# Low-rank products, token mixing, key norms and bonus sums move into the input projection of a one-core decoder step

## What is computed

```python
h = rmsnorm(x, norm1) * (1 + sc1) + sh1
proj = h @ w_in                       # 2048 x 5656
p_rkv = proj[..., RKV_OFF:GATE_OFF]   # 3 x 1024 columns; p_rkv_prev is the row before
rkv = p_rkv + mu_rkv * (p_rkv_prev - p_rkv)
r, k, v = split(rkv, 3)
xx = h_shift - h                      # h_shift: the row before, state_shift for the first
xw, xa, xg = (h + xx * mu_wag[i] for i in range(3))
w_log = -softplus(-(decay_w0 + tanh(xw @ decay_w1) @ decay_w2)) - 0.5
decay = exp(-exp(w_log))
a = sigmoid(iclr_a0 + (xa @ iclr_a1) @ iclr_a2)
g = sigmoid(xg @ gate_g1) @ gate_g2
kk = heads(k * k_k); kk = kk / max(sqrt(sum(kk * kk)), 1e-12)
k = k * (1 + (a - 1) * k_a)
# scan over tokens with r, decay, k, v, kk, a; then
bonus = sum(r * k * r_k, per head) * v
```

## Time and profile before

| | us |
|---|---|
| median of 3 runs | 2838.94 (2838.39 to 2849.66) |
| profiled execution, own time | 2834.51 |
| its span, first to last instruction | 2832.1 |
| mean granted TensorE clock | 0.902 |

### The profile page before, as it was taken

One profiled execution on the slowest core, in us unless ns is written; L12 is line 12 of the kernel. 1 busy time (PEld: TensorE's weight loads), 2 busy tenths in 40 slices (PEclk: granted clock), 3 DMA queues, 4 the chain that ended last, 5 costly groups with the idle time before them and its releaser, 6 DMA issues. The chain is left out here.

```text
span 2832.1 us, 48973 instructions
## 1 busy us (share of the span) xinstructions
PE 2373.7 (84%) x21091; PEld 1728.0 (61%) x21091; DVE 780.7 (28%) x1996; ACT 297.8 (11%) x681; POOL 77.9 (3%) x119
## 2 busy tenths in 40 slices
PE   5999998599999536776576698689999999999996
PEld 4677676377777426674564476556656666566664
DVE  0211211300000584445466502411211221112215
ACT  0101100100000210001142200100100011100001
POOL 0000000000000100000101100100000000000000
PEclk9999999599999756767588899699999999999998
DMA  5888884433331312001376820699999999999991
GB/s 213 336 303 311 338 301 183 165 117 121 118 119 59 63 41 96 5 5 34 67 229 241 314 107 1 271 425 422 427 417 425 426 422 426 418 423 427 421 420 54
DMA packets 182404, 687.45 MB, mean 243 GB/s; under 512 B 38810, under 2 KB 39787, under 8 KB 142667
## 3 DMA queue, kind: packets, MB, share of 16 engines
q1 hardware_dynamic: 172002, 640.42, 57.5%
q0 software_dynamic: 7056, 38.29, 4.0%
q10 hardware_dynamic: 3220, 6.86, 0.6%
HBM read 687.09 MB, written 19.86 MB: 250 GB/s over the span
## 5 line engine op out<-in xcount | busy, mean ns | idle before, releaser
L2498 PE MATMUL bank<-sb_gate_w,sb_x_picked 128*64 128x256 f32 x2048 | 331.6, 389 | 51.4 <-DMA sb_up_w<-in_w_up_dram 51.4
L571 PE MATMUL bank<-sb_hT,sb_w_in 128*128 128x296 f32 x1408 | 353.7, 415 | 3.9 <-PEq L462 3.9
L2498 PE MATMUL bank<-sb_up_w,sb_x_picked 128*64 128x256 f32 x2048 | 330.7, 388 | 0.0
L571 PEld LDWEIGHTS bank<-sb_hT,sb_w_in 128*128 128x128 f32 x1408 | 269.0, 191 | 88.6 <-issue 6.0
L2498 PEld LDWEIGHTS bank<-sb_gate_w,sb_x_picked 128*64 128x64 f32 x2048 | 175.9, 140 | 122.7 <-issue 78.2
L2523 PE MATMUL bank<-sb_down_w,sb_hiddenT 128*64 128x512 f32 x1024 | 226.8, 594 | 9.0 <-ACT sb_x_picked L2580 9.0
L397 PE MATMUL bank<-sb_cmp_xT,sb_cmp_w 128*128 128x254 f32 x1024 | 223.4, 379 | 6.7 <-ACT sb_cmp_xT L213 5.8
L397 PEld LDWEIGHTS bank<-sb_cmp_xT,sb_cmp_w 128*128 128x128 f32 x1024 | 193.2, 190 | 39.0 <-ACT sb_cmp_xT L213 8.4
L2498 PEld LDWEIGHTS bank<-sb_up_w,sb_x_picked 128*64 128x64 f32 x2048 | 179.5, 140 | 49.1 <-issue 0.6
L2650 DVE TENSOR_TENSOR sb_hidden<-sb_hidden,bank 128x256 f32<-128x256 f32 x32 | 13.5, 421 | 679.4 <-ACT sb_hidden L2588 679.4
L2523 PEld LDWEIGHTS bank<-sb_down_w,sb_hiddenT 128*64 128x64 f32 x1024 | 84.1, 137 | 128.9 <-issue 115.4
(11 more groups left out here) (543 smaller groups left out, 2480.1 us busy)
## 6 DMA issues: line engine op xcount, KB each, us to landing
sb_gate_w<-in_w_gate_dram SPq DMA_DIRECT2D x64, 2048.0 KB, 16.6
sb_up_w<-in_w_up_dram SPq DMA_DIRECT2D x64, 2048.0 KB, 20.9
sb_down_w<-in_w_down_dram SPq DMA_DIRECT2D x64, 2048.0 KB, 17.7
sb_w_ada<-in_w_ada_dram SPq DMA_DIRECT2D x48, 2048.0 KB, 10.8
sb_w_in<-in_w_in_dram SPq DMA_DIRECT2D x11, 4096.0 KB, 13.2
sb_cmp_raw<-in_cache_cmp_kv_dram SPq DMA_DIRECT2D x128, 256.0 KB, 7.6
sb_sample_kv<-in_w_out_dram SPq DMA_DIRECT2D x16, 1024.0 KB, 11.1
sb_sample_kv<-in_state_win_kv_dram SPq DMA_DIRECT2D x8, 1024.0 KB, 13.8
```

The source lines that it names most:

```text
L571: ins = pe.matmul(k.bank[m][:, 0:NX], w[r][:, t, m * P:(m + 1) * P], k.hT[:, t, :], start=(t == 0), stop=(t == KT - 1))
L2498: ins = pe.matmul(bank[b][64 * half:64 * half + 64, col:col + 256], x[:, t, b * 64:b * 64 + 64], w[i][:, t % CK, half * 256:half * 256 + 256],
```

## The change

`phase_lora`, `phase_rkv` and the last-rows block go; their work moves into `phase_in`, whose stage now ends at the scan.

- Weight chunks have 256 columns (2 MB, two tiles), still in two buffers; the 24 r, k, v tiles come first, the other 20 after, with 288 columns.
- Mixing h before a product is replaced by scaling the matrix: x @ W with x = (1 - mu) h + mu h_shift becomes h @ ((1 - mu) W) plus the shifted columns of h @ (mu W). DVE scales the down matrices, PE does four groups of 16 products, DVE adds the shifted part.
- For r, k, v ACT writes (1 - mu) times the tile, DVE adds mu times the neighbouring columns straight from PSUM.
- High products, sums of squares, bonus sums and the branch gates stand between tiles in PE's list; key norms, reciprocals and bonus run one tile of 288 columns at a time on ACT and DVE.
- The samples' states are loaded into the first weight buffer once its last tiles are done, and transposed at the end of the stage. The scan's masks run in the same stage.
- Buffers are shared with tiles that are not in use yet. 39 semaphores more belong to the set that `phase_rows` clears.

The core of the diff:

```diff
+def w_in_column(n):
+    blocks = RKV_TILE // 2
+    return (n + blocks if n < 3 * RT // 2 else n - 3 * RT // 2) * 2 * P
...
+                sp.dma_start(r1[0][:, :, 0:64], view("decay_w1")).then_inc(s_l1, 16)
+                sp.dma_start(r1[0][:, :, 64:128], view("iclr_a1")).then_inc(s_l1, 16)
+                sp.dma_start(r1[1], view("gate_g1")).then_inc(s_l1, 16)
+                for tile, name in zip(w2, ("decay_w2", "iclr_a2", "gate_g2")):
+                    sp.dma_start(tile, A[name][0]).then_inc(s_l2, 16)
+                sp.wait_ge(s_lr, 4)
+                sp.dma_start(A["shift_prompt"][0], last_rows[0:1, :]).then_inc(s_lo, 16)
+                sp.dma_start(A["shift_sample"][0], last_rows[1:NC, :]).then_inc(s_lo, 16)
+                for n in range(2, N_CH):
+                    sp.wait_ge(s_tile, 2 * n - 2)
+                    sp.dma_start(w[n % 2][:, :, :], w_view[:, :, w_in_column(n):w_in_column(n) + 2 * P]).then_inc(s_w[n % 2], 16)
+                    if n == 2:
+                        sp.dma_start(wg[:, :, :], w_view[:, :, GATE_OFF:IN_W]).then_inc(s_wg, 16)
+                sp.wait_ge(s_tile, N_T - 2)
+                for b in range(NB):
+                    sp.dma_start(k.state_rows[b // 2][64 * (b % 2):64 * (b % 2) + 64, :].rearrange("i (h j) -> i h j", j=64),
+                                 A["state_wkv"][0, b].rearrange("h i j -> i h j")).then_inc(s_states, 16)
...
+                def tile(j):
+                    n, ch = j // 2, k.w_in[j // 2 % 2]
+                    pe.wait_ge(s_w[n % 2], 16 * (n // 2 + 1))
+                    if 4 <= j < N_R + 4:
+                        pe.wait_ge(s_mix, j - 3)
+                    elif j >= N_R + 4:
+                        pe.wait_ge(s_copy[j % 2], (j - 4 - N_R) // 2 + 1)
+                    wide = NX if j < N_R else NT
+                    for t in range(KT):
+                        ins = pe.matmul(bank[j % 4][:, 0:wide], ch[:, t, j % 2 * P:(j % 2 + 1) * P], hT[:, t, 0:wide],
+                                        start=(t == 0), stop=(t == KT - 1))
+                    ins.then_inc(s_tile, 1)
...
+                def low_rank():
+                    pe.wait_ge(s_lr, 4)
+                    for i in range(4):
+                        pe.wait_ge(s_wm, i // 2 + 1)
+                        wide = NX if i % 2 else NT
                         for t in range(KT):
+                            ins = pe.matmul(bank[4 + i][:, 0:wide], (r1, m1)[i % 2][i // 2][:, t, :], hT[:, t, 0:wide],
                                             start=(t == 0), stop=(t == KT - 1))
...
+                def squares_summed(t):
+                    pe.wait_ge(s_sq, t + 1)
+                    pe.wait_ge(s_ha, 2 * RT)
+                    pe.wait_ge(s_hd, RT)
+                    if t >= 4:
+                        pe.wait_ge(s_mx, t - 3)
+                    pe.matmul(bank[4 + t % 4][:, 0:NT], k.headones[:, :], k.bonus[:, t, :], start=True, stop=True).then_inc(s_n, 1)
...
+                def states_turned():
+                    pe.wait_ge(s_states, 16 * NB)
+                    pe.wait_ge(s_gc, len(ROWS))
+                    for p in range(2):
+                        pe.wait_ge(s_copy[p], (N_T - N_R) // 2)
+                    for pair in range(NB // 2):
+                        for t in range(RT):
+                            ins = pe.transpose(bank[2 * pair + t // 4][:, (t % 4) * P:(t % 4 + 1) * P],
+                                               k.state_rows[pair][:, t * P:(t + 1) * P], k.ident[:, :])
+                        ins.then_inc(s_turned, 1)
+                for j in range(N_T):
+                    tile(j)
+                    if j == 0:
+                        last_turned()
+                    elif j == 3:
+                        low_rank()
+                    elif 8 <= j < 20:
+                        high(2 * (j - 8))
+                        high(2 * (j - 8) + 1)
+                    elif 20 <= j < 28:
+                        squares_summed(j - 20)
+                    elif 30 <= j < 38:
+                        bonus_summed(j - 30)
+                    elif j == 40:
+                        branch_gates()
+                states_turned()
...
+                def own_part(j):
+                    act.wait_ge(s_tile, j + 1)
+                    act.activation(k.rkvT[:, j, 0:NT], bank[j % 4][:, 0:NT], ACT.Copy, scale=om[:, j:j + 1]).then_inc(s_ev, 1)
...
+                def keys(t):
+                    act.wait_ge(s_mix, RT + t + 1)
+                    kk_gain = k.par[:, C_KK + t:C_KK + t + 1]
+                    act.activation(k.kk[:, t, :], K[:, t, :], ACT.Copy, scale=kk_gain)
+                    act.activation(k.bonus[:, t, :], K[:, t, :], ACT.Square, scale=kk_gain).then_inc(s_sq, 1)
+                    act.activation(k.y[:, t, :], k.a[:, t, :], ACT.Identity, bias=oka[:, t:t + 1],
+                                   scale=k.par[:, C_KA + t:C_KA + t + 1]).then_inc(s_t2, 1)
+                def root(t):
+                    act.wait_ge(s_mx, t + 1)
+                    act.activation(k.y[:, t, :], k.y[:, t, :], ACT.Sqrt).then_inc(s_rt, 1)
...
+                for j in range(N_T):
+                    if j < N_R:
+                        own_part(j)
+                    elif j % 2 == 0:
+                        act.wait_ge(s_tile, j + 1)
+                        act.copy(k.pT[:, j - N_R, 0:NT], bank[j % 4][:, 0:NT]).then_inc(s_copy[0], 1)
+                    if j == 3:
+                        low_copied()
+                    elif j == 5:
+                        low_activated()
+                    elif 8 <= j < 16:
+                        rates(2 * (j - 8))
+                        rates(2 * (j - 8) + 1)
+                    if j == 16:
+                        act.wait_ge(s_ha, 2 * RT)
+                        act.activation(k.dec[:, :, :], k.dec[:, :, :], ACT.Exp, scale=-0.6065306597126334)
+                    if 16 <= j < 24:
+                        keys(j - 16)
+                    elif 24 <= j < 32:
+                        root(j - 24)
...
+                def mixed(j):
+                    dve.wait_ge(s_ev, j + 1)
+                    out, ps, mu = k.rkvT[:, j, :], bank[j % 4], k.par[:, C_MURKV + j:C_MURKV + j + 1]
+                    how = dict(scalar=mu, op0=ALU.mult, op1=ALU.add)
+                    dve.scalar_tensor_tensor(out=out[:, 1:TP], in0=ps[:, 0:TP - 1], in1=out[:, 1:TP], **how)
+                    rest = by_sample(out[:, TP:NT])[:, :, 1:TS]
+                    dve.scalar_tensor_tensor(out=rest, in0=by_sample(ps[:, TP:NT])[:, :, 0:TS - 1], in1=rest, **how)
+                    dve.scalar_tensor_tensor(out=out[:, TP:NT:TS], in0=ps[:, NT:NX], in1=out[:, TP:NT:TS], **how).then_inc(s_mix, 1)
...
+                def weights_scaled(i):
+                    dve.wait_ge(s_l1, 48)
+                    for lo, col in (((0, C_MUWAG), (64, C_MUWAG + KT)), ((0, C_MUWAG + 2 * KT),))[i]:
+                        hi = lo + (64, P)[i]
+                        ins = dve.tensor_tensor(m1[i][:, :, lo:hi], r1[i][:, :, lo:hi],
+                                                k.par[:, col:col + KT].unsqueeze(2).to_broadcast([P, KT, hi - lo]), ALU.mult)
+                    step(ins)
+                    dve.tensor_tensor(r1[i], r1[i], m1[i], ALU.subtract).then_inc(s_wm, 1)
...
+                def key_scaled(t):
+                    dve.wait_ge(s_t2, t + 1)
+                    dve.tensor_tensor(K[:, t, :], K[:, t, :], k.y[:, t, :], ALU.mult).then_inc(s_k, 1)
+                def bounded(t):
+                    dve.wait_ge(s_k, t + 1)
+                    dve.wait_ge(s_n, t + 1)
+                    dve.tensor_scalar(k.y[:, t, :], bank[4 + t % 4][:, 0:NT], 1e-24, None, ALU.max).then_inc(s_mx, 1)
+                    dve.scalar_tensor_tensor(out=k.bonus[:, t, :], in0=R[:, t, :], scalar=k.par[:, C_RK + t:C_RK + t + 1],
+                                             in1=K[:, t, :], op0=ALU.mult, op1=ALU.mult).then_inc(s_bq, 1)
+                def normed(t):
+                    dve.wait_ge(s_rt, t + 1)
+                    step(dve.reciprocal(k.y[:, t, :], k.y[:, t, :]))
+                    step(dve.tensor_tensor(k.kk[:, t, :], k.kk[:, t, :], k.y[:, t, :], ALU.mult))
+                    dve.tensor_tensor(k.a[:, t, :], k.a[:, t, :], k.kk[:, t, :], ALU.mult)
+                def bonus(t):
+                    dve.wait_ge(s_bn, t + 1)
+                    dve.tensor_tensor(k.bonus[:, t, :], bank[4 + t % 4][:, 0:NT], V[:, t, :], ALU.mult).then_inc(s_bo, 1)
...
+                for j in range(N_T):
+                    if j < N_R:
+                        mixed(j)
+                    elif j % 2:
+                        dve.wait_ge(s_tile, j + 1)
+                        dve.tensor_copy(k.pT[:, j - N_R, 0:NT], bank[j % 4][:, 0:NT]).then_inc(s_copy[1], 1)
+                    if j == 0:
+                        dve.wait_ge(s_lt, 1)
+                        for q in range(4):
```

(77 more changed lines are left out.)

298 lines of the change are left out of this document (78 added, 220 removed).

## The result

The changed kernel takes 2761.09 us (median, 2757.40 to 2762.29), the kernel before beside it on the same chip 2838.66 (2831.19 to 2849.66): a ratio of 0.9717, 95% interval 0.9694 to 0.9741. The forecast was 2762, in a range of 2746 to 2782.

The account below looks back on a forecast made before the run. The path was taken as PE in the projection, then a load, then DVE, 501.0 us; PE's summed work starts the scan 77.0 us earlier, so 2834.5 becomes 2757.5, plus 4.4 for the median: 2762 us, range 2746 to 2782.

Parts of the forecast that it names:

- the sum: Merged projection stage: PE's work added up as if nothing waited, 416.6 us plus borders and tail; scan starts 77.0 us earlier.
- Low-rank products: Merged stage: four groups of 16 products on PE in place of three, 128 records, 31.4 us.
- The last rows' transposes: Right behind the first tile: 16 transposes on PE at full clock, 2.2 us, between 2.2 and 3.6.
- The tail: After the last tile: copy out, 32 state transposes (4.4 us), last copy and stage border, 6.3 us until the scan.
- Gates and restart: Between tiles 40 and 41: branch gates 12.5 us, then 2.6 us lost as tile 41 starts at 1.2 GHz.
- Borders: PE's list in the merged stage: some 40 borders between small groups, 1 us in all, bounds 0 and 5.
- Loads: Weight chunks of 2 MB land in 8 us (6 to 13), hidden in at least 15.5 us of two tiles.
- the tightest cover: Stage end: eight state loads of 14.5 us hidden under tiles 42 and 43, 15.5 to 18 us; loss up to 14.5.
- An uncovered wait: Rival in PE's queue: exposed state rows +14.5 us (2776), late low-rank weights +15.5 (2778), both 2792; chance 0.11.
- Chunk loads set the pace: Rival at 20 later chunks: 20 us for each us over 15.5, slower beyond 19.3; chance 0.05, slower 0.03 of it.
- No overlap: Rival in the merged stage: helpers too slow for the tiles, DVE work returns, up to 64 us, 2826; chance 0.02.
- A larger gain: Rival in scan and gates: scan keeps 2.4 GHz for a while, gates may stay fast, 5 to 15 us; chance 0.08.

Follow-up runs that it names:

- e5: Changed kernel with two more DVE products of 2304 columns, result thrown away, in each of the 44 tiles: one run, 2757.24 us.
- e2: Changed kernel with the branch gates' operands exchanged, so 288 columns move instead of 24, plus three small transposes: 2758.63 us, ratio to before 0.9725.
- e8: Changed kernel with every weight chunk from the third on loaded three times in a row: one run, 2854.37 us.
- e3: Changed kernel with matrix scaling undone: DVE mixes the 48 inputs under tiles 0 to 3, PE does three product groups, not four: 2753.07 us, ratio to before 0.9711.
- e9: Kernel before with only the weight chunks changed, to 256 columns from 512: 2842.63 us, ratio to before 0.9999.
- e10: Version with both edits, plus 24 thrown-away PE products ahead of the first tile: 2758.56 us, ratio to before 0.9696.
- e12: Version with both edits, plus 27 thrown-away PE products ahead of the first tile: 2750.38 us, ratio to before 0.9687.
- the version with both edits: Changed kernel with gate operands exchanged and inputs mixed once on DVE, run twice: 2743.74 and 2744.57 us, ratios to before 0.9674 and 0.9654.

## Why the prediction was right

**What bounds, and the sum.** The step that carries the forecast, PE's work added up with nothing waiting, held: 424.0 us from the end of the norm to the scan were summed, 422.7 measured; the scan was put at 974.4 and starts at 974.41, since a first tile 1.2 us late made up for it. This agreement to 0.01 us is chance, and so in part is the one of 2762 with 2761.09: the sum gave 2757.5 for the profiled execution, which took 2760.75, as the attention was 6.4 us longer and the scan 3.1 shorter, and the 4.4 us that were added for the median of the runs happened to cover that. The changed kernel's own runs go from 2747.82 to 2762.29. Low-rank products 31.4 against 618.55 - 587.08 = 31.5. The last rows' transposes 2.2 against 1.91. The tail was put 1 us too long, 6.3 against 974.41 - 969.07 = 5.3: its transposes took 3.68 us for 4.4.

**Gates and restart.** 12.5 and 2.6 against 11.04 and 25.59 - 96 x 0.2415 = 2.4; the gates' 12.5 us is within what they take from run to run (12.92 in e5). The choice to follow the row and not idleness as the cause was right in kind: 9.1 us and no loss behind them did not come, and e2 shows why.

**Borders** were the one term undersized: 1 us, within its bounds of 0 and 5. Taking the other terms out of the 417.4 us leaves some 2.6, or 3.5 if one counts that the first tile happened to be 0.9 us shorter than the one inside the 353.3 us (9.89 for 10.8). The high products with 64 rows of weights are enough for that: in the timeline of the changed kernel a tile and a pair of them take 9.34 us from tile to tile, with 128 rows 8.94, and there are eight such pairs (3.2 us):

```profile
659.67 8.24 PE L588 MATMUL bank<-sb_hT,sb_w_in 128*128 128x296 f32 x32
667.84 1.24 PE L615 MATMUL bank<-sb_low_wa,sb_pT 64*128 64x288 f32 x4
669.01 8.24 PE L588 MATMUL bank<-sb_hT,sb_w_in 128*128 128x296 f32 x32
...
743.01 8.14 PE L588 MATMUL bank<-sb_hT,sb_w_in 128*128 128x296 f32 x32
750.98 1.13 PE L615 MATMUL bank<-sb_low_g,sb_pT 128*128 128x288 f32 x4
751.95 8.14 PE L588 MATMUL bank<-sb_hT,sb_w_in 128*128 128x296 f32 x32
```

**Loads.** 8 us were taken for a chunk from bounds of 6 and 13; it lands in 8.2. No wait for low-rank weights or state rows either: these were asked for at 953.55, 16.1 us ahead of their first transpose, and the last of them moved before 967.5, with some 2 us to spare. That load was the tightest cover on paper; no run here made it later.

**Rivals.** *An uncovered wait*: none, the two waits above are all. *Chunk loads set the pace*: refuted here, but e8 shows the mechanism and that it can end slower than before; its price of 20 us for each us over 15.5 was too dear, since the cover is nearer 17.7. *No overlap*: refuted, and e5 shows room for two DVE products of 2304 columns in each tile, but for 3 us at the stage's end. *A larger gain*: not shown; the scan took 302.8 us for 305.9, at the same clock of 0.70 and within its scatter.

**What the forecast did not see** is that one of the change's parts costs time. The cost of the scaled matrices was counted rightly: 31.4 us for four groups. But their other side, the mixing of inputs on DVE (23.2 us before), would have been free under the tiles, and e3 shows the 7.6 to 8.8 us that the trade gives away. The gain of the change is nearly all overlap: 69.5 of the 78.3 us are idle time of PE, the size of the chunks gives nothing by itself (e9), and the scaling takes some of the gain back. The 288 columns for 296 in 20 tiles, 4.7 us by the sum, were not run alone.

## What to carry to other kernels

When stages are merged under one busy engine, sum that engine's work and then check each helper and load against the time between its request and its use; work that is moved onto the busy engine to relieve an idle one is paid in full. Judge a small edit by the stretch that it touches where the rest of the program scatters by more than its worth, and look for the part of the stretch that scatters too. An idle gap ahead of dense matrix work (here 3.09 us or more), or a run of products with few moving columns, can be paid again in the tiles behind it.

## What was not expected of the hardware

- A busy PE can lose its clock: 0.68 over the gates with 24 moving columns, 0.59 in the 5.2 us of tiles behind them, with no idle time; 1.00 with 288 columns (e2).
- An idle 3.09 us behind dense work cost as much as an idle 14.7 us, and 1.65 us cost nothing (e10, e12, one profile each).
- Behind the same idle 14.7 us the first tile takes 9.69 to 11.22 us; the rest of the stretch repeated to 0.1 us in two profiles of the changed kernel and in two of the version with both edits.
- The attention takes 267.1 to 286.5 us from one execution to the next, with the same instructions. Why is open; no run here went into it.
